# Placing, loading and addressing the expert weights of a mixture of experts in another way

## The chip, the cores and the metric

The kernel runs on one core of one Trainium2 chip. The metric is the device time of one execution in microseconds (us). Engines: PE is TensorE, PEld its weight loads, DVE VectorE, ACT ScalarE, POOL GpSimd, SP SyncE, whose queue issues most transfers.

## The reference, cut to what matters

One layer over 16 meta tokens and 1024 tokens of width 1024: an S5 mixer, an HGRN2 mixer and differential attention side by side, an output projection, and a hierarchical mixture of experts (4 groups of 4 experts, the two best of one group for each token). The change touches only the last:

```python
for e in range(MOE_EXPERTS):                       # 16, of width MOE_FF = 512
    he = jax.nn.silu(t @ w_gate[e]) * (t @ w_up[e])
    y = y + gates[:, e:e + 1] * (he @ w_down[e])   # gates is zero but for two experts of a token
```

All is float32. One expert has 2 MB each of gate, up and down weights.

## The kernel before

**Slots and blocks.** The 2048 pairs of token and chosen expert are sorted by expert into blocks of P = 128 slots, so that a block has one expert and an expert one block or more. The number of blocks depends on the data; the program allows for up to NB, and here 24 run. Functions `..._experts` hold one instruction stream for each engine. `blocks(eng, body)` writes bodies 0 and 1 out, loops over pairs of bodies (j is the pair, par the block in it, b = 2j + par) and writes the last pair out.

**One body.** Body b computes the gate and up products of block b+1 and then the down products of block b. Weights are cut into chunks of 128 rows and 1024 columns: 8 for gate and up (gate and up side by side), 4 for down, so a body has 12 places. float32 products are made of three fp32r products, x_high w_high + x_low w_high + x_high w_low. For each chunk ACT casts the high part (`higher`, L2323), DVE (`lower`, L2375) or POOL (L2220) subtracts it for the low part, and PE (`product`, L2277) does 3 x 2 matmuls of 512 columns. The parts lie in a ring of RING = 4 places; ACT casts a chunk when the chunk four before it has been used (semaphore `chunk_used`). POOL has the last of four chunks (places 3, 7 and 11), DVE the others.

Within a body PE turns the hidden rows (four transposes, L2302), does gate and up, turns the gathered rows of block b+2 (eight transposes, L2257), and does down. ACT then applies SiLU (L2332) and copies the high parts of x (L2328); DVE multiplies gate and up (`hidden`, L2393), takes the low parts of x (L2381) and of the hidden rows (L2442) and scales the outputs of block b-1 (L2401). POOL gathers the rows of block b+2 from DRAM (L2204 and L2207), copies three columns of indices (L2213 to L2215) and adds the outputs of block b-1 into DRAM by a scatter (L2247); DVE's L2401 waits until the scatter before has landed.

**Weights.** There are two places for an expert's weights, `WGU` and `WDN`; an expert that comes new takes the other one. Experts 0 and 1 are loaded ahead. For every block SP reads six table entries: expert, place, whether the expert is new, and three values of `chunk_used` at which the first half of gate and up, the second half and down are free. It then issues five transfers at addresses made of registers, which are skipped where the expert is not new. The other engines that read weights take the places of blocks b and b+1 from a table at the head of each body:

```python
e, q, new, free, free_second, free_down = (sp.value_load(tab[0:1, bass.ds(b, 1)], min_val=0, max_val=hi)
                   for tab, hi in ((eblk, NE - 1), (ebuf, 1), (enew, 1), (efree, 12 * NB), (efree2, 12 * NB), (edown, 12 * NB + 12)))
...
q = buffer_of(eng, b)
return q, (buffer_of(eng, b + 1) if has(par, last, 1) else None)
```

DVE makes the tables in `dve_route` (L2008 to L2041) once the routing is known. The first 8 x 1024 columns of SBUF hold the routing's work and, after the last body, the residual rows.

## Time and profile before

| | us |
|---|---|
| median of 3 runs | 1196.25 |
| the runs | 1192.59 to 1198.74 |
| span of the profiled execution, first to last instruction | 1192.0 |
| experts, body 0 to the end of the last down product | 723.73 to about 1162 |
| PE busy in the span | 1065.8 |
| DVE, ACT, POOL busy | 843.0, 638.6, 487.2 |

The profiled execution is one more execution, of which the trace gives the span and no time of its own; the span is 0.6 us below the fastest run and 4.25 below the median.

How to read the rows: a timeline row has start, time in us, engine, line, operation, output<-input, count; rows of one engine and line that follow closely are merged. In brackets stands the idle time ahead of it and who ended it. A row of windows has start and end, length, then the busy time and instructions of PE, PEld, DVE, ACT and POOL, the granted PE clock as a share of full speed, the mean busy share of the 16 DMA engines and GB/s. A row of a source line has count, then minimum, median and maximum in ns. A row of waits has total us, times, longest.

### The profile page before, as it was taken

To read this page: it belongs to the slowest core of one execution; us is meant where nothing else is said; L and a number is where in the kernel's file an instruction comes from. 1 tells how busy PE (TensorE), PEld (TensorE's weight loads), DVE (VectorE), ACT (ScalarE), POOL (GpSimd) and SP (SyncE) were. 2 spreads that over 40 slices of the span, in tenths; PEclk is the share of its full clock that TensorE was granted. 3 is DMA by queue.
4 is the path that set the end of the run, shared out by engine and by line. 5 is a ranking of instruction groups with operands and counts; after the bars stand their busy time and mean duration, and the time that the engine had idled before them with its cause. 6 is when DMAs were issued, how large, how long until landed. Compare 5 with 4: busy or idle time off the path is not lost. (4 is left out here: it accounts for less than half of the span.)

```text
span 1192.0 us, 22049 instructions
## 1 busy us (share of the span) xinstructions
PE 1065.8 (89%) x7126; PEld 888.2 (75%) x7126; DVE 843.0 (71%) x1234; ACT 638.6 (54%) x1008; POOL 487.2 (41%) x303
## 2 busy tenths in 40 slices
PE   4899998999969989999999648999999999999995
PEld 4898998889968646666667536878777887888873
DVE  5797857563357556555554497888887999899987
ACT  5522111166533456444443326778776887888854
POOL 1121211122000226111111114878775887999960
PEclk9999999999988989999999859999999999999988
DMA  7216434332033820011111774788999878877454
GB/s 266 80 48 73 118 95 127 102 114 71 21 72 80 319 71 1 19 54 53 54 66 59 280 267 159 238 257 305 322 379 371 275 266 286 258 266 229 103 160 161
DMA packets 89495, 194.97 MB, mean 164 GB/s; under 512 B 9265, under 2 KB 32049, under 8 KB 88769
## 3 DMA queue, kind: packets, MB, share of 16 engines
q1 hardware_dynamic: 82800, 169.91, 42.0%
q0 software_dynamic: 6624, 24.12, 8.5%
q8 instruction: 45, 0.74, 0.3%
q14 instruction: 26, 0.20, 0.1%
HBM read 220.60 MB, written 31.51 MB: 211 GB/s over the span
## 5 line engine op out<-in xcount | busy, mean ns | idle before, releaser
L2277 PE MATMUL ps<-split 128*128 128x512 f32 x1728 | 418.1, 398 | 15.8 <-DVE split L2375 8.1
L2277 PEld LDWEIGHTS ps<-split 128*128 128x128 f32 x1728 | 322.4, 190 | 93.3 <-DVE split L2375 12.8
L2323 ACT CAST split<-weights 128x1024 fp32r (+1 forms) x288 | 298.2, 1052 | 101.9 <-PE ps L2277 80.4
L2375 DVE TENSOR_TENSOR split<-weights,split 128x1024 fp32r<-128x1024 f32 x216 | 300.9, 1446 | 46.5 <-ACT split L2323 45.0
L480 PE MATMUL ps<-xsplit,wsplit 128*128 128x384 f32 (+2 forms) x1440 | 239.7, 324 | 4.0 <-POOL wsplit L252 4.0
L2220 POOL TENSOR_TENSOR split<-weights,split 128x1024 fp32r<-128x1024 f32 x72 | 205.0, 2847 | 91.4 <-ACT split L2323 90.4
L480 PEld LDWEIGHTS ps<-xsplit,wsplit 128*128 128x128 f32 x1440 | 226.2, 189 | 5.4 <-POOL wsplit L252 4.6
L252 POOL TENSOR_TENSOR wsplit<-mem,wsplit 128x1024 fp32r<-128x1024 f32 x22 | 57.1, 2597 | 247.7 <-ACT wsplit L335 247.7
L1605 DVE TENSOR_REDUCE sml<-ps 128x1 f32<-128x1040 f32 (+7 forms) x64 | 46.6, 769 | 61.6 <-PE ps L1785 61.6
L1722 ACT COPY mem<-ps 128x512 f32<-128x512 f32 (+3 forms) x48 | 21.4, 481 | 109.3 <-PE ps L1804 71.7
L1548 POOL TENSOR_TENSOR sml<-sml 128x4 f32<-128x4 f32 x8 | 8.1, 1015 | 156.2 <-DVE sml L1626 156.2
L335 ACT CAST wsplit<-mem 128x1024 fp32r<-128x1024 f32 x22 | 23.2, 1053 | 85.1 <-DMA mem<-in_w_in 85.1
L2247 POOL DMA_INDIRECT h_d<-par,sml x22 | 53.0, 2408 | 3.4 <-issue 3.0
L1661 ACT ACTIVATE mem<-ps,sml 128x1040 f32<-128x1040 f32 (+7 forms) x64 | 47.1, 736 | 0.0
L1810 PE MATMUL ps<-mem 128*128 128x128 f32 x288 | 39.3, 282 | 7.1 <-ACT mem L1722 7.1
L2207 POOL DMA_INDIRECT con<-xn_d,sml x24 | 37.7, 1571 | 19.3 <-POOL sml L2204 19.3
L1810 PEld LDWEIGHTS ps<-mem 128*128 128x128 f32 x288 | 34.7, 191 | 12.6 <-ACT mem L1722 12.2
L1785 PE MATMUL ps<-mem 64*128 64x400 f32 (+6 forms) x224 | 42.4, 493 | 0.0
L419 ACT COPY mem<-ps 128x384 f32<-128x384 f32 (+2 forms) x48 | 20.3, 451 | 40.9 <-PE ps L480 34.6
L2328 ACT CAST split<-ps 128x512 fp32r<-128x512 f32 x48 | 25.7, 589 | 17.8 <-PE ps L2257 17.8
L1026 POOL TENSOR_TENSOR sml<-sml 128x16 f32<-128x16 f32 x2 | 7.6, 3800 | 66.6 <-DVE sml L1231 66.6
L2401 DVE TENSOR_SCALAR par<-ps,sml 128x512 f32<-128x512 f32 x44 | 30.9, 744 | 5.1 <-DMA h_d<-par,sml 5.1
(434 smaller groups left out, 1631.1 us busy)
## 6 DMA issues: line engine op xcount, KB each, us to landing
weights<-in_w_down SPq DMA_DIRECT2D x26, 2048.0 KB, 15.9
weights<-in_w_gate SPq DMA_DIRECT2D x50, 1024.0 KB
weights<-in_w_up SPq DMA_DIRECT2D x50, 1024.0 KB
mem<-in_w_in SPq DMA_DIRECT2D x22, 512.0 KB, 4.4
mem<-in_x SPq DMA_DIRECT2D x10, 512.0 KB, 3.5
mem<-in_w_out SPq DMA_DIRECT2D x1, 4096.0 KB, 14.8
h_d<-mem SPq DMA_DIRECT2D x8, 512.0 KB, 2.6
xn_d<-mem SPq DMA_DIRECT2D x8, 512.0 KB, 2.6
```

What stands on the lines that cost most here:

```text
L252: nc.gpsimd.tensor_tensor(WLO[i], RAW[i], WHI[i].bitcast(F32), ALU.subtract).then_inc(wlo_ready, 1)
L480: mm = nc.tensor.matmul(ps[:, n % 6, 0:hi - lo], w[slot_of(h)][:, k % 4, P * m:P * m + P], x[:, k, lo:hi], start=(k == 0 and p_ == 0), sto ...
L1605: nc.vector.tensor_reduce(NMX[:, 2 * (n % 2) + c:2 * (n % 2) + c + 1], logits(c)[:, KEY0:KEY0 + keys_of(n)], AX.X, ALU.max, negate=True).t ...
L1661: f(PR_[n % 2][:, c, 0:nk], logits(c)[:, KEY0:KEY0 + nk], ACT.Exp, bias=NMX[:, o:o + 1], accum_out=SUM[:, o:o + 1]).then_inc(exp_done, 1)
L1785: mm = nc.tensor.matmul(logits(c)[:, s:e], AQ[R, h, P * i:P * i + P], AK[R, h, s - lo:e - lo], start=(e != hi), stop=True, skip_group_chec ...
L1810: nc.tensor.matmul(b[:, 0:P], AT[n % 2][:, k], V[:, 1 + k, vc], start=(k == 0), stop=False)
L2207: pool.indirect_dma_start(XG[:, par], None, xn_d, bass.IndirectOffsetOnAxis(ap=ixc[:, par:par + 1], axis=0)).then_inc(xg_loaded[par], 16)
L2220: nc.gpsimd.tensor_tensor(WL[place % RING], raw(kind, k, q), WH[place % RING].bitcast(F32), ALU.subtract).then_inc(wl_pool, 1)
L2247: pool.indirect_dma_start(h1_d, bass.IndirectOffsetOnAxis(ap=sixc[:, 1 - par:2 - par], axis=0), YE, None, compute_op=ALU.add).then_inc(ye_ ...
L2277: mm = nc.tensor.matmul(ps[:, bank + h, :], x, w[place % RING][:, 512 * h:512 * h + 512], start=(k == 0 and p_ == 0), stop=(k == n - 1 and ...
L2323: nc.scalar.copy(WH[place % RING], raw(kind, k, q)).then_inc(wh_ready, 1)
L2375: nc.vector.tensor_tensor(WL[place % RING], raw(kind, k, q), WH[place % RING].bitcast(F32), ALU.subtract).then_inc(wl_dve, 1)
```

## The change

Gate and up weights get three places, expert e at place e mod 3; the third is the first 8 x 1024 columns of SBUF. Down weights keep two, by parity of e. SP loads every expert's weights in the order of e, at fixed addresses and never skipped: gate and up of e+1, then down of e. It reads one table entry for each expert, the value of `chunk_used` at which half of its gate and up weights have been used in its last block. Every expert gets at least one block.

ACT, DVE and POOL read the place of gate and up from one table (`gtab`, in units of 128 columns) and that of down from another (`dtab`), and ACT the expert (`etab`), since the semaphores of the loads now count experts. DVE and ACT read at the head of a body only where par is 0; the rest is read before place ASK = 6 and place 9, and handed on to the next body in `known`. The first AHEAD = 3 chunks of block 1 are cast and subtracted before the SiLU of block 0.

```diff
 SPLIT = 5 * D + RING * 2 * D
+O_RING = NT * D + 5 * D
+UNIT = 128
+GU_AT = (O_C, O_C + 2 * KD * FF, 0)
...
+        etab, half_free, npair = sml[:, 506:506 + NB].bitcast(I32), sml[:, 398:398 + NE].bitcast(I32), sml[:, 504:505].bitcast(I32)
+        gtab, dtab = sml[:, 570:570 + NB].bitcast(I32), sml[:, 366:366 + NB].bitcast(I32)
         rt_exp, onehot_ready, rank_done, slots_ready, tables_ready, slot_hot_ready, idx_done = (
...
-            link(ts(BLK[:, 0:2], BLK[:, 0:2], 1.0, None, ALU.max))
+            link(ts(BLK, BLK, 1.0, None, ALU.max))
...
-            link(nc.vector.tensor_copy(eblk[:, :], EBF))
-
-            scan = nc.vector.tensor_tensor_scan
-            link(nc.vector.memset(NEW[:, 0:1], 1.0))
-            link(tt(NEW[:, 1:NB], EBF[:, 1:NB], EBF[:, 0:NB - 1], ALU.not_equal))
...
-            link(tt(OLD, OLD, NEW, ALU.subtract))
-            link(scan(BUF, OLD, NEW, 1.0, ALU.mult, ALU.add))
-            link(nc.vector.tensor_copy(ebuf, BUF))
+            link(nc.vector.tensor_copy(etab, EBF))
+            link(tt(ECMP, ECMP, con[:, C_GUB:C_GUB + NE].unsqueeze(1).to_broadcast([P, NB, NE]), ALU.mult))
+            link(red(GUF, ECMP, AX.X, ALU.add))
+            link(ts(GUF, GUF, float(GU_AT[0] // UNIT), None, ALU.add))
+            link(nc.vector.tensor_copy(gtab, GUF))
+            link(ts(PARITY, EBF, 0.5, -0.25, ALU.mult, ALU.add))
...
+            link(nc.vector.tensor_copy(dtab, PARITY))
+            link(tt(PCMP, CB[:, NE - 1:NE].to_broadcast([P, (NB - LEAST) // 2]), con[:, C_IOTAB + LEAST:C_IOTAB + NB:2], ALU.is_gt))
...
+            nc.vector.tensor_copy(half_free, CB).then_inc(tables_ready, 1)
             dve_rows_lower(dve, 0, 0)
-            link(stt(NEW, EBF, 1.5, NEW, ALU.is_gt, ALU.mult))
...
-        WGU = weights[:, 0:4 * KD * FF].rearrange("p (k i n) -> p k i n", i=2, n=FF)
+        WGU = gate_up[:, O_C:].rearrange("p (k i n) -> p k i n", i=2, n=FF)
         WDN = weights[:, 4 * KD * FF:].rearrange("p (k n) -> p k n", n=D)
+        GATE_UP = gate_up[:, :].rearrange("p (a n) -> p a n", n=UNIT)
+        CHUNK = 2 * FF // UNIT
...
-                return WGU[:, bass.ds(q * KD + k, 1)].rearrange("p a i n -> p (a i n)")
+                return GATE_UP[:, bass.ds(q + CHUNK * k, CHUNK)].rearrange("p a n -> p (a n)")
...
+            for half in range(2):
+                sp.sem_inc(w_loads[half], 32)
             sp.wait_ge(xg_loaded[0], 16)
-            sp.dma_start(WDN[:, FF // P:2 * FF // P], a["w_down"][1].rearrange("(k p) n -> p k n", p=P)).then_inc(wdn_loaded, 16)
             sp.wait_ge(first_loaded, 48)
+            sp.sem_inc(wdn_loaded, 16)
+            sp_down(sp, 1)
             sp.wait_ge(tables_ready, 1)
-
-            def body(j, par, first, last):
-                b = 2 * j + par
-                e, q, new, free, free_second, free_down = (sp.value_load(tab[0:1, bass.ds(b, 1)], min_val=0, max_val=hi)
-                                   for tab, hi in ((eblk, NE - 1), (ebuf, 1), (enew, 1), (efree, 12 * NB), (efree2, 12 * NB), (edown, 12 * NB + 12)))
-                for half in range(2):
-                    sp.wait_ge(w_loads[half], 32 * b + 32)
-                    sp.wait_ge(chunk_used, (free, free_second)[half])
-                    for i, w in enumerate(("w_gate", "w_up")):
-                        sp.dma_start(WGU[:, bass.ds(q * KD + 4 * half, 4), i],
-                                     a[w][bass.ds(e, 1), 512 * half:512 * half + 512].rearrange("a (k p) n -> p (a k) n", p=P),
-                                     cond=new).then_inc(w_loads[half], 16)
-                sp.wait_ge(wdn_loaded, 16 * b + 16)
-                sp.wait_ge(chunk_used, free_down)
-                sp.dma_start(WDN[:, bass.ds(q * (FF // P), FF // P)], a["w_down"][bass.ds(e, 1)].rearrange("a (k p) n -> p (a k) n", p=P),
-                             cond=new).then_inc(wdn_loaded, 16)
-
-            return blocks(sp, body)
-
-        def buffer_of(eng, b):
-            return eng.value_load(ebuf[0:1, bass.ds(b, 1)], min_val=0, max_val=1)
-
-        def buffers(eng, b, par, last):
-
-            q = buffer_of(eng, b)
-            return q, (buffer_of(eng, b + 1) if has(par, last, 1) else None)
+            sp.wait_ge(slots_ready, 2)
+            sp_gate_up(sp, 2, None)
+            free = sp_half_free(sp, 0)
+            for e in range(2, NE):
+                if e + 1 < NE:
+                    free_next = sp_half_free(sp, e - 1)
+                    sp_gate_up(sp, e + 1, free)
+                sp_down(sp, e, free)
+                free = free_next
+            pairs = sp.value_load(npair[0:1, 0:1], min_val=0, max_val=(NB - LEAST) // 2) + LEAST // 2
+            return pairs
+
+        def sp_half_free(sp, e):
+
+            return sp.value_load(half_free[0:1, e:e + 1], min_val=12 + gu_used(-1) - KD // 2, max_val=12 * NB)
+
+        def sp_gate_up(sp, e, free):
+
+            for half in range(2):
+                sp.wait_ge(w_loads[half], 32 * e)
+                if free is not None:
+                    if e == 3:
+                        sp.wait_ge(chunk_used, gu_used(0))
+                    sp.wait_ge(chunk_used, free + KD // 2 * half)
+                at = GU_AT[e % 3] + 4 * half * 2 * FF
+                place = gate_up[:, at:at + 4 * 2 * FF].rearrange("p (k i n) -> p k i n", i=2, n=FF)
+                for i, w in enumerate(("w_gate", "w_up")):
+                    sp.dma_start(place[:, :, i], a[w][e, 512 * half:512 * half + 512].rearrange("(k p) n -> p k n", p=P)).then_inc(w_loads[half], 16)
+
+        def sp_down(sp, e, free=None):
+
+            sp.wait_ge(wdn_loaded, 16 * e)
+            if free is not None:
+                sp.wait_ge(chunk_used, free + (down_used(1, False) - gu_used(1) + KD // 2))
+            k = FF // P * (e % 2)
+            sp.dma_start(WDN[:, k:k + FF // P], a["w_down"][e].rearrange("(k p) n -> p k n", p=P)).then_inc(wdn_loaded, 16)
+
+        def expert_of(eng, b):
+            return eng.value_load(etab[0:1, bass.ds(b, 1)], min_val=0, max_val=NE - 1)
+
+        def gate_up_place(eng, b):
+            return eng.value_load(gtab[0:1, bass.ds(b, 1)], min_val=min(GU_AT) // UNIT, max_val=max(GU_AT) // UNIT)
+
+        def down_place(eng, b):
+            return eng.value_load(dtab[0:1, bass.ds(b, 1)], min_val=0, max_val=1)
+
+        ASK = 6
...
-                q, q_next = buffers(pool, b, par, last)
+                q_next = gate_up_place(pool, b + 1) if has(par, last, 1) else None
                 if par and last:
+                    q = down_place(pool, b)
...
+                    if place == KD:
+                        q = down_place(pool, b)
...
+            act.wait_ge(tables_ready, 1)
+            q_first, e_first = gate_up_place(act, 1), expert_of(act, 1)
+            act.wait_ge(w_loads[0], 32 * e_first + 32)
+            act.sem_inc(act_seen, 1)
+            for place in range(AHEAD):
+                higher(0, place, "gu", place, q_first)
             silu(0, 0)
-            act.wait_ge(tables_ready, 1)
             copy_x(1, 1)
 
             def body(j, par, first, last):
                 b = 2 * j + par
-                q, q_next = buffers(act, b, par, last)
+                if par:
+                    e, q_next, e_next, q = known
+                elif first:
+                    q_next, e_next = q_first, e_first
+                else:
+                    q_next, e_next = gate_up_place(act, b + 1), expert_of(act, b + 1)
                 for place, (kind, k) in enumerate(chunks(not has(par, last, 1))):
+                    if first and not par and place < AHEAD:
+                        continue
+                    if place == ASK and has(par, last, 1):
+                        if not par:
+                            e = expert_of(act, b)
+                        q = down_place(act, b)
+                    if place == ASK + 3 and not par:
+                        known[:] = (e_next, None, None, None)
+                        if last:
+                            known[3] = down_place(act, b + 1)
+                        else:
+                            known[1:3] = gate_up_place(act, b + 2), expert_of(act, b + 2)
                     if kind == "gu" and k % 4 == 0:
-                        act.wait_ge(w_loads[k // 4], 32 * b + 96)
+                        act.wait_ge(w_loads[k // 4], 32 * e_next + 32)
                         act.sem_inc(act_seen, 1)
                     if (kind, k) == ("down", 0):
-                        act.wait_ge(wdn_loaded, 16 * b + 32)
+                        act.wait_ge(wdn_loaded, 16 * e + 16)
...
+            q_first = gate_up_place(dve, 1)
+            for place in range(AHEAD):
+                lower(0, place, "gu", place, q_first)
             hidden(0, 0)
             x_lower(1, 1)
             dve_slot_tables(dve, link)
 
             def body(j, par, first, last):
                 b = 2 * j + par
-                q, q_next = buffers(dve, b, par, last)
+                if par:
+                    q_next, q = known
+                else:
+                    q_next = q_first if first else gate_up_place(dve, b + 1)
                 for place, (kind, k) in enumerate(chunks(not has(par, last, 1))):
-                    if place % RING < RING - 1:
+                    if place == ASK and has(par, last, 1):
+                        q = down_place(dve, b)
+                    if place == ASK + 3 and not par:
+                        known[:] = (None, down_place(dve, b + 1)) if last else (gate_up_place(dve, b + 2), None)
+                    if place % RING < RING - 1 and not (first and not par and place < AHEAD):
```

## Rows read from the trace of the kernel before

**Rows 1.** The page, part 1: busy time of TensorE in the span.

```profile
PE 1065.8 (89%) x7126; PEld 888.2 (75%) x7126; DVE 843.0 (71%) x1234; ACT 638.6 (54%) x1008; POOL 487.2 (41%) x303
```

**Rows 2.** Windows, cut where bodies begin, bodies 0 to 21.

```profile
723.73:745.81 22.08, 18.55 (x84) 14.63 (x85) 19.16 (x20) 17.04 (x19) 11.03 (x7) 1.00 0.55 192
745.81:781.91 36.10, 35.99 (x170) 29.30 (x169) 31.70 (x31) 28.52 (x33) 30.92 (x18) 1.00 0.81 272
781.91:801.95 20.04, 18.32 (x85) 14.57 (x84) 16.36 (x16) 14.45 (x17) 13.02 (x10) 1.00 0.70 197
801.95:855.16 53.21, 53.21 (x253) 44.19 (x252) 46.33 (x45) 42.31 (x49) 44.92 (x28) 1.00 0.89 306
855.16:933.90 78.74, 74.33 (x338) 58.00 (x337) 64.06 (x61) 56.18 (x65) 51.88 (x37) 1.00 0.97 340
...
987.50:1008.63 21.13, 18.66 (x86) 14.49 (x85) 19.87 (x17) 14.46 (x17) 14.42 (x10) 1.00 0.96 342
...
sum 409.60, PE 397.36 PEld 321.98 DVE 357.65 ACT 317.73 POOL 325.84; mean PE 49.67 PEld 40.25 DVE 44.71 ACT 39.72 POOL 40.73
```

**Rows 3.** Waits of ScalarE, 704 to 1150 us.

```profile
ACT split L2323 <- DMA weights<-in_w_up: 16.3, 5, 3.8
```

**Rows 4.** Timeline of body 7.

```profile
855.57 0.38 SPq L2185 DMA_DIRECT2D weights<-in_w_down  x1
...
860.52 0.39 SPq L2180 DMA_DIRECT2D weights<-in_w_gate  x1
...
861.16 1.04 ACT L2323 CAST split<-weights 128x1024 fp32r x1 [3.70 <-DMA weights<-in_w_up]
```

**Rows 5.** Source line of SyncE's table reads.

```profile
L2174 SPq TENSOR_LOAD <-sml x144: 261/267/1300, 710.2 to 1101.8; - x144
```

**Rows 6.** Windows: body 8 alone.

```profile
875.07:894.76 19.69, 18.56 (x85) 14.50 (x84) 16.21 (x17) 13.90 (x17) 12.90 (x10) 1.00 1.05 375
```

**Rows 7.** Timeline of ScalarE, end of block 0's gate and up.

```profile
716.77 1.28 ACT L2332 ACT_TABLE_LOAD   x1
721.07 0.60 ACT L2332 ACTIVATE mem<-ps 128x512 f32<-128x512 f32 x1 [3.01 <-PE ps L2277]
...
723.52 1.05 ACT L2323 CAST split<-weights 128x1024 fp32r x1 [0.89 <-issue]
```

**Rows 8.** Timeline of body 0.

```profile
726.32 5.70 DVE L2375 TENSOR_TENSOR split<-weights,split 128x1024 fp32r<-128x1024 f32 x3 [1.44 <-ACT split L2323]
...
727.59 3.04 PE L2277 MATMUL ps<-split 128*128 128x512 f32 x12 [1.73 <-DVE split L2375]
```

**Rows 9.** Source line of VectorE's subtractions.

```profile
L2375 DVE TENSOR_TENSOR split<-weights,split x216: 1208/1218/3432, 685.5 to 1151.9; 128x1024 fp32r<-128x1024 f32 x108
```

**Rows 10.** Timeline of body 14.

```profile
987.02 5.71 DVE L2375 TENSOR_TENSOR split<-weights,split 128x1024 fp32r<-128x1024 f32 x3 [1.35 <-ACT split L2323]
...
989.20 2.44 POOL L2220 TENSOR_TENSOR split<-weights,split 128x1024 fp32r<-128x1024 f32 x1
```

**Rows 11.** Timeline of body 18.

```profile
1061.21 3.50 DVE L2375 TENSOR_TENSOR split<-weights,split 128x1024 fp32r<-128x1024 f32 x3 [1.32 <-ACT split L2323]
...
1063.54 3.44 POOL L2220 TENSOR_TENSOR split<-weights,split 128x1024 fp32r<-128x1024 f32 x1 [0.22 <-ACT split L2323]
```

**Rows 12.** Source line of the other engines' table reads.

```profile
L2191 DVEq FUSED_REGOPS  x69: 65/190/216, 725.2 to 1147.1; - x69
...
L2191 ACTq TENSOR_LOAD <-sml x47: 273/283/1185, 721.9 to 1145.3; - x47
...
L2191 DVEq TENSOR_LOAD <-sml x47: 298/312/1617, 724.6 to 1146.7; - x47
```

**Rows 13.** Timeline of body 3.

```profile
785.96 1.41 DVE L2401 TENSOR_SCALAR par<-ps,sml 128x512 f32<-128x512 f32 x2 [2.03 <-DMA h_d<-par,sml]
```

**Rows 14.** Waits, all engines, 704 to 1140 us.

```profile
PEld ps L2277 <- POOL split L2220: 5.3, 13, 0.6
```

**Rows 15.** Source line of one table operation.

```profile
L2010 DVE TENSOR_SCALAR mem<-mem x1: 181/181/181, 702.6 to 702.6; 128x32 f32<-128x32 f32 x1
```

More of the change, by code:

```diff
@@ L50 @@
 C_TOK, C_DESC4, C_128J, C_SG, C_IOTAB = 896, 912, 928, 936, 937
-C_COS = 976
+C_GUB = 976
+C_COS = 992
 C_SIN = C_COS + L
@@ L90, in constants @@
     c[:, C_IOTAB:C_IOTAB + NB] = np.arange(NB)
+    place = np.array([GU_AT[e % len(GU_AT)] // UNIT for e in range(NE)])
+    c[:, C_GUB:C_GUB + NE - 1] = place[1:] - place[:-1]
     inv = (np.float32(1.0) / (np.float32(10000.0) ** (np.arange(0, 64, 2, dtype=np.float32) / np.float32(64)))).astype(np.float32)
@@ L129, in build @@
             split, weights = split_tensor, weights_tensor
+        with nc.sbuf_tensor("gate_up", [P, O_C + 4 * KD * FF], F32) as gate_up_tensor:
+            gate_up = gate_up_tensor
         with (nc.sbuf_tensor("below_x", [P, O_X], F32), nc.sbuf_tensor("xsplit", [P, 2 * KD * L], F32R) as xsplit_tensor,
@@ L141, in build @@
         MLOE_T = split_at("mix_early_lower", MEM - 512, 512)
+        WHIGH_T, WLOW_T = split_at("weights_higher", O_RING, RING * D), split_at("weights_lower", O_RING + RING * D, RING * D)
         WOL_T = [split_at("wo_lower%d" % k, O_C + 2 * KD * FF + 1024 * k, 1024) for k in range(KD)]
@@ L1878, in build @@
         CB, ECMP, EBF, IXF = take(NE), take(NB, NE), take(NB), take(NB)
-        NEW, OLD, RUN, PRV, BUF, NHALF, NPR = take(NB), take(NB), take(NB), take(NB), take(NB), take(1), take(1)
-        PCMP = take(NB // 2)
+        NPR, PCMP, GUF, PARITY = take(1), take((NB - LEAST) // 2), take(NB), take(NB)
         assert oS <= NT * D
@@ L1886, in build @@
         ixb, ixc = sml[:, 538:538 + NB].bitcast(I32), sml[:, 602:604].bitcast(I32)
-        eblk, ebuf, enew = (sml[:, o:o + NB].bitcast(I32) for o in (506, 570, 398))
-        efree2 = sml[:, 104:104 + NB].bitcast(I32)
-        efree, edown, npair = sml[:, 366:366 + NB].bitcast(I32), sml[:, 334:334 + NB].bitcast(I32), sml[:, 504:505].bitcast(I32)
+        etab, half_free, npair = sml[:, 506:506 + NB].bitcast(I32), sml[:, 398:398 + NE].bitcast(I32), sml[:, 504:505].bitcast(I32)
+        gtab, dtab = sml[:, 570:570 + NB].bitcast(I32), sml[:, 366:366 + NB].bitcast(I32)
         rt_exp, onehot_ready, rank_done, slots_ready, tables_ready, slot_hot_ready, idx_done = (
@@ new lines, in dve_route @@
+            link(ts(GUF, GUF, float(GU_AT[0] // UNIT), None, ALU.add))
+            link(nc.vector.tensor_copy(gtab, GUF))
+            link(ts(PARITY, EBF, 0.5, -0.25, ALU.mult, ALU.add))
+            link(ts(PARITY, PARITY, MAGIC, None, ALU.add))
+            link(ts(PARITY, PARITY, -MAGIC, None, ALU.add))
+            link(nc.vector.scalar_tensor_tensor(PARITY, PARITY, -2.0, EBF, ALU.mult, ALU.add))
+            link(nc.vector.tensor_copy(dtab, PARITY))
+            link(tt(PCMP, CB[:, NE - 1:NE].to_broadcast([P, (NB - LEAST) // 2]), con[:, C_IOTAB + LEAST:C_IOTAB + NB:2], ALU.is_gt))
@@ L2043, in dve_slot_hot @@
+            link(red(NPR, PCMP, AX.X, ALU.add))
+            link(nc.vector.tensor_copy(npair, NPR))
+            link(ts(CB, CB, 12.0, float(gu_used(-1) - KD // 2), ALU.mult, ALU.add))
+            nc.vector.tensor_copy(half_free, CB).then_inc(tables_ready, 1)
+            dve_rows_lower(dve, 0, 0)
         def dve_slot_hot(dve, link):
@@ L2085, in build @@
         HH, HLO = (take_split(FF).rearrange("p (k q) -> p k q", k=FF // P) for _ in range(2))
-        WH, WL = ([take_split(D) for _ in range(RING)] for _ in range(2))
+        WH, WL = ([v[:, r * D:r * D + D] for r in range(RING)] for v in (WHIGH_T, WLOW_T))
+        assert oS == O_RING
+        take_split(2 * RING * D)
         SG, HE = take(FF), take(FF)
@@ L2124, in build @@
         USED0 = 5
+        AHEAD = 3
         def gu_used(b):
@@ L2328, in copy_x @@
                     nc.scalar.copy(XH[:, par, 4 * h:4 * h + 4], ps[:, 6 + h, :].rearrange("p (k q) -> p k q", k=4)).then_inc(xh_ready, 1)
+            known = [None] * 4
             def silu(b, par):
@@ L2422, in tokens_of_slots @@
                                             ALU.is_equal).then_inc(slot_rows_ready, 1)
+            known = [None] * 2
             dve_slot_hot(dve, link)
```

21 lines of the change are left out of this document (removed).

## The prediction

> **What bounds the kernel now.** The page's first part comes first: TensorE is busy for 89% of the span [rows 1]. The change touches only the mixture of experts, so the second view is a table of windows over the first 22 of its 24 bodies (one body per block of 128 slots), cut where the transposes of a body begin [rows 2]. Three bodies in a row took 53.21 us with TensorE busy for all of it: 17.74 us is what a body costs when nothing is late. The 22 bodies from 723.73 to 1133.33 took 409.60 us; 22 x 17.74 = 390.28 would do, and 19.3 us are stalls. They sit in few places: body 0 took 22.08 (4.34 too much), body 3 20.04 (2.30), bodies 7 to 10 78.74 (7.78), body 14 21.13 (3.39). The other fifteen hold the remaining 1.5. That is the most the change can win there, and each piece has a cause of its own.
>
> **Bodies 7 to 10: transfers.** Before its casts ScalarE waited 16.3 us in five pieces for gate and up weights [rows 3]. In body 7 the second half's cast started at 861.16 after 3.70 us of such a wait, and SyncE issued that body's loads, down at 855.57 and the next gate and up at 860.52 [rows 4]. The 5 us between them are register reads, 144 in 24 bodies, six for each [rows 5]. In body 8 the DMA share is full (1.05) at 375 GB/s [rows 6]; 375 GB/s x 19.69 us = 7.4 MB, which is one expert's 6.3 MB with the gathered and scattered rows. Here each expert has one block, so every body needs 7.4 MB, 19.7 us of transfer against 17.74 of work. No order of issue makes that shorter. But the deficit is only 1.95 us a body, 7.8 in four bodies, and the bodies ahead of it have free transfer time (share 0.70 in body 3, 0.89 in bodies 4 to 6 [rows 2]). With a third place, gate and up of expert e+1 wait for expert e-2 and not for e-1: one body, 17.74 us, more lead. 17.74 is more than 7.8, so the whole deficit fits. The static order keeps down(e) behind gate_up(e+1), and down(e) waits for the end of the last body of e-2; it is needed 11.5 us into the first body of e, with singles one body and 11.5 us = 29 us after its release, against 19.7 us for all that is queued with it. I take 0.3 left: minus 7.5 us (bounds 0 and 7.8).
>
> **Body 0: first chunks of block 1 ahead of SiLU.** ScalarE now loads its table at 716.77 while it waits, starts SiLU at 721.07, copies x, and casts the first chunk of the second block at 723.52 after 0.89 us in its sequencer [rows 7]. VectorE's subtractions follow at 726.32, three in 5.70 us, and TensorE stands 1.73 us till 727.59 and again later [rows 8]. After: three casts and three subtractions are done while TensorE still works on block 0, so the 4.34 us go. What is late next is SiLU. A chunk of six matmuls takes (17.74 - 1.0) / 12 = 1.40 us; TensorE's last but one chunk of block 0 ends near 721.0 - 1.4 = 719.6, the third early cast waits for it, starts near 719.9 and ends at 720.95. The table load stands in program order just ahead of SiLU, so its 1.28 us [rows 7] lose their cover: SiLU at 722.25, 1.2 later, and behind it in ScalarE's queue the copies of x, VectorE's lower parts and the transposes. Minus 4.34, plus 1.2: minus 3.1 us (bounds 0, if as much is lost again, and 4.3). The Trainium skill ("ScalarE: Activation LUTs", What ACT_TABLE_LOAD costs) counts a drain of 1.38 us with each load, 2.66 us in all; by it SiLU would come 2.5 late and this part would be worth 1.8. The trace has the load at 1.28 with no such time before it.
>
> **Bodies 3 and 14: two engines in each other's way.** A VectorE subtraction has a median of 1.218 us and a maximum of 3.432 [rows 9]. In body 14 the third one started at 987.02 + 5.71 - 3.43 = 989.30, just after GpSimd's own at 989.20, which took 2.44 [rows 10]: VectorE stood still till GpSimd had finished. In body 18 VectorE's third starts at 1061.21 + 3.50 - 1.22 = 1063.49, GpSimd's at 1063.54 and takes 3.44 [rows 11]; GpSimd is the one that waits and nothing stalls. So every body is a race decided by 0.1 us, and a lost one costs up to 3.4 us; body 0 holds one too (5.70 for three [rows 8]). The Trainium skill ("SBUF — State Buffer", SBUF: two separate sides) says that the first of the two to start keeps a shared port for its whole instruction and the other blocks fully; the trace agrees (3.43 against 1.22 us). Now the reads: ahead of its first subtraction VectorE was idle 1.32 us [rows 11], and its two table reads stand there (a load of 0.31 us and register work of 0.19 each [rows 12]). After the change that place has one read in even bodies and none in odd ones: the race starts 0.5 to 1.1 us earlier, bounded by the third cast, and VectorE wins it. Body 3 was also started by a scatter: VectorE waited 2.03 us for the store of the last rows [rows 13], with the transfers of expert 3 in front of it. Those are issued one body earlier now. I take minus 3.0 for body 14 (bounds 0 and 3.4) and minus 1.8 for body 3 (bounds 0 and 2.3).
>
> **The rest.** GpSimd ended a body's gate and up part too late 13 times, 5.3 us of weight loads waiting in all, most of it overlapped by running matmuls [rows 14]; its column copies are held up by VectorE, which is now earlier. Bodies 1 and 2 keep the 0.6 they lose (36.10 - 35.48, the loop's entry); of the 0.9 us left for bodies 11 to 13 and 15 to 21 I take 0.5. The tables: some 30 small VectorE operations become 18, most at 0.18 us [rows 15]; the path to TensorE's first matmul ends with the x copy, not with them: nothing, either way at most 1 us. SyncE's loads with fixed addresses exist already, at 0.4 us an issue, and nothing waits behind them; conditional ones that were skipped are gone. ScalarE reads more: seven table reads per pair of bodies for four. Each is 0.28 us of load [rows 12], with the register work of VectorE's kind about 0.5; two come between chunks 5 and 6, and the pitch there is 1.40 us with a cast of 1.05 running: they hide under the cast. Zero, bound below.
>
> **Sum.** 7.5 + 3.1 + 3.0 + 1.8 + 0.5 = 15.9 us. The profiled execution spans 1192.0, the three runs lie at 1192.59 to 1198.74 with the median 4.25 above the span; the last instruction to the run's end is not in the trace. 1192.0 - 15.9 = 1176.1 of span, and with the same 4.25 the median is 1180.35, rounded 1180.
>
> **Rivals.**
> The races stay (0.15). New reads sit before chunk 6, where VectorE meets GpSimd's chunk 7; a lost race costs 1.4 to 3.4 us. If bodies 3 and 14 are as before or two others take their place, 4.8 us fewer: 1185. For it: margins under 1 us; against: 0.1 us became more at the place that lost.
> The loads still bind (0.09). If the queue is held by a wait in SyncE's order, such as down(e) in front of gate_up(e+2), the 7.5 us stay: 1188. Against: the lead of 17.74 us over 7.8.
> The opening wins little (0.08): SiLU late by as much as is saved, 3.1 us fewer: 1183.5.
> Slower (0.06): the reads. If ScalarE's two reads, 0.5 us each, are not hidden and shift the cast that GpSimd's slow chunk 7 waits for, that is 1.0 us a body, 22 us: 1180 + 22 = 1202. The point from which it decides is 15.9 / 22 = 0.72 us exposed per body. For it: GpSimd is already the last to finish in 13 bodies; against: four chunks of lead, 4.2 us, in the ring.
> The forecast itself has 0.62.
>
> **Numbers.** Own range of the likeliest case: 1176 to 1185. Below, all 19.3 us gone and a low run: 1174. Above, the race, opening and load rivals: up to 1188, with 2 for the spread of the runs: 1190. 0.5% is 6.0 us, about what can be told from no change: faster means below 1190.3, slower above 1202.2. Faster 0.87, same 0.08, slower 0.05.
>
> **What would show it.** Right: no wait of ScalarE on gate and up weights in bodies 7 to 10, which take 17.7 to 17.9 each; SiLU of block 0 near 722.3, behind its table load, and body 0 at 17.8 to 18.2; at most one subtraction of 3.4 us in places 0 to 2; VectorE's first subtraction under 0.8 us after the x rows. Wrong: transfers at full share in a body over 19 us; idle TensorE after GpSimd's chunk 7 or ScalarE's chunk 6 in every even body.

## The result, and the profile after

The changed kernel takes 1176.1 us (median of 4 runs, 1173.4 to 1178.9) against 1195.4 (median of 4, 1192.6 to 1198.7) in the same session: a ratio of 0.984, 95% interval 0.981 to 0.988. The forecast was 1180, range 1174 to 1190.

Its profiled execution spans 1177.1 us and took 1178.9, the slowest of the four; before's spans 1192.0. The spans differ by 14.9 us, the medians by 19.3. Part of this is the code ahead of the experts, which the diff doesn't touch: the first transposes of gathered rows start at 704.71 in before and at 707.34 in after, and in the profiled executions of the experiments below between 705.7 and 709.9. So I measure **the experts' stretch**, from those transposes to the end of the span. Before it is 1192.0 - 704.71 = 487.3 us, after 1177.1 - 707.34 = 469.8: 17.5 us less.

The windows of the bodies of after, cut as [rows 2] (columns: bounds, length, busy time and instructions of PE, PEld, DVE, ACT and POOL, granted clock, DMA share, GB/s):

```profile
727.35:746.65 19.30, 19.30 (x84) 15.94 (x85) 15.65 (x17) 13.47 (x15) 9.03 (x8) 0.91 0.81 305
746.65:782.06 35.41, 35.41 (x169) 29.48 (x168) 31.26 (x31) 28.91 (x33) 28.36 (x19) 1.00 1.05 388
782.06:799.77 17.71, 17.71 (x85) 14.74 (x84) 14.81 (x16) 14.46 (x17) 12.90 (x10) 1.00 0.82 260
...
852.89:923.75 70.86, 70.86 (x338) 58.99 (x337) 62.24 (x61) 58.09 (x65) 56.85 (x37) 1.00 1.04 382
923.75:1029.96 106.21, 106.21 (x506) 88.40 (x505) 93.36 (x91) 86.80 (x97) 87.70 (x54) 1.00 0.92 315
1029.96:1049.95 19.99, 18.30 (x85) 14.58 (x84) 16.20 (x16) 14.21 (x17) 13.17 (x10) 1.00 0.52 136
1049.95:1120.78 70.83, 70.83 (x338) 58.93 (x337) 63.25 (x61) 57.79 (x65) 59.98 (x35) 1.00 0.44 119
```

Twenty of these 22 bodies take 17.71 us each, without a gap of TensorE. Bodies 7 to 10, in the fifth row, went from 78.74 to 70.86 us while the DMA share is 1.04: the transfers are as dense as before, only earlier. Bodies 3 and 14 are at 17.71 too. Two bodies are left over: body 0 (19.30), where TensorE is busy for all of the time but its clock is 0.91, and body 17 (19.99).

The waits of after, 704 to 1140 us (total, times, longest), beside [rows 3] and [rows 14]:

```profile
DVE par L2449 <- DMA h_d<-par,sml: 9.7, 10, 2.3
...
PEld ps L2301 <- DVE weights_lower L2423: 2.5, 2, 1.9
...
PE ps L2326 <- DVE split L2429: 2.1, 1, 2.1
...
ACT weights_higher L2347 <- DMA gate_up<-in_w_up: 0.2, 1, 0.2
```

ScalarE's 16.3 us of waits for gate and up weights are down to one of 0.2, TensorE's for GpSimd are gone. VectorE's wait for the scatter grew from 5.1 to 9.7 us.

The opening of after: ScalarE's timeline answers to [rows 7].

```profile
719.81 2.20 ACT L2347 CAST weights_higher<-gate_up 128x1024 fp32r x2 [0.61 <-PE ps L2301]
722.31 1.06 ACT L2347 CAST weights_higher<-gate_up 128x1024 fp32r x1 [0.30 <-PE ps L2301]
723.39 1.28 ACT L2358 ACT_TABLE_LOAD   x1
724.68 0.60 ACT L2358 ACTIVATE mem<-ps 128x512 f32<-128x512 f32 x1
```

And the windows of TensorE behind it, same columns as above:

```profile
725.00:727.00 2.00, 0.24 (x5) 0.07 (x2) 1.83 (x4) 2.00 (x4) 0.00 (x0) 1.00 0.68 160
727.00:729.00 2.00, 1.65 (x9) 1.46 (x10) 1.86 (x6) 0.78 (x2) 1.52 (x1) 0.90 0.25 102
729.00:731.00 2.00, 2.00 (x7) 1.54 (x6) 1.75 (x3) 0.91 (x1) 1.27 (x4) 0.50 0.00 0
731.00:733.00 2.00, 2.00 (x8) 1.66 (x7) 1.23 (x1) 0.62 (x2) 0.00 (x0) 0.74 0.61 202
```

The early casts stand ahead of the table load, which now has no cover. TensorE waits 2.1 us for block 1's x rows (0.9 in before), and then runs for about 3 us at half its clock, 1.2 GHz.

Body 17 in the timelines of VectorE and GpSimd:

```profile
1033.99 1.41 DVE L2449 TENSOR_SCALAR par<-ps,sml 128x512 f32<-128x512 f32 x2 [2.28 <-DMA h_d<-par,sml]
1035.32 0.68 DVE L2501 TENSOR_TENSOR split<-ps,split 128x512 fp32r<-128x512 f32 x1
1035.91 5.69 DVE L2423 TENSOR_TENSOR weights_lower<-gate_up,weights_higher 128x1024 fp32r<-128x1024 f32 x3
...
1037.57 2.95 POOL L2241 TENSOR_TENSOR weights_lower<-gate_up,weights_higher 128x1024 fp32r<-128x1024 f32 x1 [2.92 <-ACT weights_higher L2347]
```

VectorE waits 2.28 us for the scatter of the block before, comes to its three subtractions late, and the third starts while GpSimd's is running: 5.69 us for three, as in [rows 10], here at places 4 to 6. Before's body 3 lost its race at place 6 too, behind the same kind of wait [rows 13]: that race was not gone, it had moved to another body.

### The profile page after: what moved, and what is told of

The parts are those of the page before. It is cut to its first block and busy times, and to the rows that moved or that the text cites. A ratio compares the mean times of both kernels' runs of the same rounds, so it can differ in the third digit from the quotient of the medians.

```text
span 1177.1 us, 21252 instructions
## 1 busy us (share of the span) xinstructions
PE 1062.5 (90%) x7126; PEld 895.1 (76%) x7126; DVE 833.9 (71%) x1221; ACT 643.1 (55%) x1008; POOL 473.1 (40%) x303
## 3 DMA queue, kind: packets, MB, share of 16 engines
q1 hardware_dynamic: 82800, 169.92, 41.4%
HBM read 157.69 MB, written 31.51 MB: 161 GB/s over the span
## 5 line engine op out<-in xcount | busy, mean ns | idle before, releaser
L2301 PE MATMUL ps<-weights_higher,split 128*128 128x512 f32 x1152 | 317.0, 397 | 3.0 <-DVE split L2501 2.3
L2301 PEld LDWEIGHTS ps<-weights_higher,split 128*128 128x128 f32 x1152 | 215.5, 190 | 46.7 <-issue 2.6
L2347 ACT CAST weights_higher<-gate_up 128x1024 fp32r (+1 forms) x192 | 200.6, 1056 | 53.9 <-PE ps L2301 48.8
L2423 DVE TENSOR_TENSOR weights_lower<-gate_up,weights_higher 128x1024 fp32r<-128x1024 f32 x144 | 178.8, 1288 | 15.6 <-ACT weights_higher L2347 14.3
L2301 PE MATMUL ps<-weights_lower,split 128*128 128x512 f32 x576 | 180.0, 394 | 1.7 <-DVE weights_lower L2423 1.7
L2241 POOL TENSOR_TENSOR weights_lower<-gate_up,weights_higher 128x1024 fp32r<-128x1024 f32 x48 | 119.1, 2482 | 76.8 <-ACT weights_higher L2347 75.5
L2301 PEld LDWEIGHTS ps<-weights_lower,split 128*128 128x128 f32 x576 | 109.4, 190 | 26.0 <-DVE weights_lower L2423 2.5
L2423 DVE TENSOR_TENSOR weights_lower<-weights,weights_higher 128x1024 fp32r<-128x1024 f32 x72 | 109.5, 1572 | 26.7 <-ACT weights_higher L2347 26.7
L2347 ACT CAST weights_higher<-weights 128x1024 fp32r x96 | 101.3, 1055 | 31.2 <-PE ps L2301 30.1
L2241 POOL TENSOR_TENSOR weights_lower<-weights,weights_higher 128x1024 fp32r<-128x1024 f32 x24 | 64.1, 2670 | 13.9 <-ACT weights_higher L2347 13.4
L1819 PE MATMUL ps<-mem 128*128 128x128 f32 x288 | 39.3, 282 | 7.1 <-ACT mem L1731 7.1
```

The source lines that it names most:

```text
L1819: nc.tensor.matmul(b[:, 0:P], AT[n % 2][:, k], V[:, 1 + k, vc], start=(k == 0), stop=False)
L2241: nc.gpsimd.tensor_tensor(WL[place % RING], raw(kind, k, q), WH[place % RING].bitcast(F32), ALU.subtract).then_inc(wl_pool, 1)
L2301: mm = nc.tensor.matmul(ps[:, bank + h, :], x, w[place % RING][:, 512 * h:512 * h + 512], start=(k == 0 and p_ == 0), stop=(k == n - 1 and ...
L2347: nc.scalar.copy(WH[place % RING], raw(kind, k, q)).then_inc(wh_ready, 1)
L2423: nc.vector.tensor_tensor(WL[place % RING], raw(kind, k, q), WH[place % RING].bitcast(F32), ALU.subtract).then_inc(wl_dve, 1)
```

## Experiments

Each row: median, ratio to before with its interval, experts' stretch of the profiled execution, and the bodies that took over 18.3 us. The runs behind one median spread over 2 to 13 us. The stretch leaves out the code ahead of the experts, but it comes from one execution of each kernel, and how far it varies between executions is not shown. Body 5 shows that it can: it takes 19.46 us in e8 and 17.7 in after, e2 and e3, though e8 differs from these in the opening alone.

| kernel | us | ratio | stretch | long bodies |
|---|---|---|---|---|
| before | 1195.4 | | 487.3 | 0, 2, 3, 7 to 10, 14 |
| after | 1176.1 | 0.981 to 0.988 | 469.8 | 0, 17 |
| e1 two places | 1181.0 | 0.982 to 0.992 | 474.1 | 0, 7, 9, 10 |
| e2 nothing ahead | 1178.3 | 0.982 to 0.990 | 469.7 | 0, 17 |
| e3 table early | 1176.7 | 0.977 to 0.988 | 469.4 | 17 |
| e4 reads at head | 1188.0 | 0.992 to 0.997 | 480.5 | 0, 4, 5, 13, 16, 17, 19 to 21 |
| e5 before, GpSimd waits | 1218.1 | 1.011 to 1.022 | 510.7 | 18 of 22 |
| e6 after, GpSimd waits | 1184.3 | 0.988 to 0.996 | 477.4 | 3, 5, 7, 17 |
| e7 both of e3, e6 | 1184.1 | 0.989 to 0.994 | 476.8 | 3, 5, 17 |
| e8 table early, nothing ahead | 1177.9 | 0.980 to 0.990 | 470.3 | 0, 5, 17 |
| e9 scatter first | 1174.1 | 0.977 to 0.987 | 467.3 | 0 |
| e10 scatter and table | 1170.1 | 0.975 to 0.983 | 464.4 | none |
| e11 VectorE's reads at head | 1178.2 | 0.981 to 0.991 | 475.2 | 0, 5, 17, 20 |
| e12 ScalarE's reads at head | 1190.1 | 0.993 to 0.999 | 483.1 | 0, 4, 5, 13, 16, 17, 19 to 21 |

**Is it the third place, or the static issue?**

```diff
-GU_AT = (O_C, O_C + 2 * KD * FF, 0)
+GU_AT = (O_C, O_C + 2 * KD * FF)
...
+                sp_down(sp, e, free)
                 if e + 1 < NE:
                     free_next = sp_half_free(sp, e - 1)
-                    sp_gate_up(sp, e + 1, free)
-                sp_down(sp, e, free)
+                    sp_gate_up(sp, e + 1, free_next)
...
-                at = GU_AT[e % 3] + 4 * half * 2 * FF
+                at = GU_AT[e % 2] + 4 * half * 2 * FF
```

> The kernel after, with its gate and up weights back in two places (block e in place e mod 2, loads still static and in the order down(e), then gate and up (e+1), each behind the product that frees its place). If the third place is what removed the stalls of bodies 7 to 10, those four bodies and body 3 go back from 17.7 us to 19 to 20 us each, ScalarE or GpSimd or VectorE wait for their transfers again, and the kernel is 6 to 9 us slower than after. If the gain came from the static issue without register reads on SyncE, the bodies stay at 17.7 us and the time is within 1 us of after.

4.9 us slower than after in the medians. ScalarE's waits in it, 704 to 1140 us:

```profile
ACT weights_higher L2347 <- DMA gate_up<-in_w_up: 11.8, 7, 5.0
```

Bodies 7, 9 and 10 take 21.60, 19.48 and 18.74 us, 6.7 more than in after; body 3 stays at 17.71. e1 still issues its loads at fixed addresses and without the reads, so what makes bodies 7 to 10 short is the third place with the order of transfers that goes with it, not the static issue. For bodies 3 and 8 (17.71 too) the expectation failed.

**What did casting ahead bring?** e2 sets AHEAD = 0. e3 loads the table early, e8 does both:

```diff
             copy_x(0, 0)
+            nc.scalar.activation(SG[:, 0:1], con[:, C_ONES:C_ONES + 1], ACT.Silu)
```

> The kernel after, with no chunks of the second block cast ahead of SiLU. If casting ahead is what shortened body 0, that body goes back from 19.3 us to about 22 us, the table load and SiLU come about 2 us earlier, and the total is 1.5 to 3 us longer than after. If casting ahead paid little, because TensorE's wait for SiLU and the lower granted clock behind it (0.91 over body 0) took back what it gave, the total is within 1 us of after.

> The kernel after, with a SiLU of one column, of constants, put on ScalarE behind its first x copy, so that the table is loaded while TensorE still has products of block 0 to do. If TensorE's 2.1 us of idle before the first hidden transposes is what lets its clock fall, the 1.28 us of table load leave that wait, it is 0.8 to 1.0 us, the granted clock of body 0 is 1.00 and the body takes 17.8 us instead of 19.3: 2.5 to 3 us less in all. If the clock falls for another reason, body 0 stays at 19.3 us and only up to 1.2 us are won.

> The kernel after, with the table loaded early and no chunks cast ahead. If casting ahead pays 2 us once the granted clock holds, the stretch from the first x transposes to the end of body 0 takes 39 us here, against 37.3 us with both, 39.3 us in after and 39.2 us with neither. If the early table alone made the gain and the casts ahead pay nothing, it takes 37 to 38 us.

From the first transposes to the end of body 0: before 41.1 us, after 39.3, e2 39.2, e8 39.2, e3 37.3. Body 0 of e3, and of e2:

```profile
729.47:747.17 17.70, 17.70 (x85) 14.76 (x85) 14.73 (x17) 13.47 (x15) 8.22 (x8) 1.00 0.85 321
```

```profile
726.90:747.43 20.53, 18.32 (x84) 14.61 (x85) 19.43 (x20) 16.04 (x18) 10.55 (x7) 1.00 0.94 348
```

Without casts ahead VectorE's race of [rows 8] is back (5.70 us for three subtractions) and body 0 takes 20.53; with them it is 19.3, but the late SiLU and the clock take it all back. With the table loaded early both are avoided and the casts ahead are worth 1.9 us. The early table alone (e8 against e2) brings nothing. e3 failed in one point: TensorE's wait fell only from 2.10 to 1.85 us, not to 0.9, since VectorE's three subtractions ahead (ending at 727.5) now hold its own multiplication back. In the stretch e3 is only 0.4 us shorter than after, because its body 17 took 21.58 us and not 19.99; the medians don't tell the two apart.

Why body 0 of e2 is 1.5 us shorter than that of before, I did not test.

**Whose reads matter?** e4 puts all table reads of ScalarE and VectorE back at the head of each body, e11 VectorE's alone, e12 ScalarE's alone. For ScalarE:

```diff
-                if par:
-                    e, q_next, e_next, q = known
-                elif first:
+                q, e = down_place(act, b), expert_of(act, b)
+                if first and not par:
                     q_next, e_next = q_first, e_first
-                else:
+                elif has(par, last, 1):
                     q_next, e_next = gate_up_place(act, b + 1), expert_of(act, b + 1)
...
```

> The kernel after, with all table reads of ScalarE and of VectorE back at the head of each body (GpSimd's stay where they are). If spreading them is what lets VectorE start its subtraction ahead of GpSimd's, VectorE's first subtraction of a body begins about 1.3 us later, some bodies show its 3.4 us form in places 0 to 2 and take 19 to 21 us, and the total is 1 to 7 us longer. If the place of the reads doesn't matter, all bodies stay at 17.7 us and the time is within 0.5 us of after.

> The kernel after, with the table reads of VectorE alone back at the head of its bodies. With both engines' reads there it was 12 us slower than after. If VectorE's late first subtraction, coming under GpSimd's, is the cost, most of it stands here: 8 to 12 us slower than after, with bodies of 18 to 20 us. If ScalarE's late first cast is the cost, this kernel is within 2 us of after.

> The kernel after, with the table reads of ScalarE alone back at the head of its bodies. If VectorE's late first subtraction is the cost of the kernel with both, this one is within 2 us of after; if ScalarE's late first cast is, which makes VectorE and GpSimd late together, it is 8 to 12 us slower.

e4 is 12 us slower than after, more than expected. e12 alone is 14 us slower (stretch 13.3 more), e11 2 us (stretch 5.4 more, by body 20 at 21.05 above all). So most of the cost of e4 comes by ScalarE's reads and not, as I had expected, by VectorE's. But e12 is no return to before: it has four reads of ScalarE at the head, where before had two. e11 does take VectorE back to before's two reads, and its body 20 is before's body 14 over again:

```profile
1084.67 2.01 ACT L2347 CAST weights_higher<-gate_up 128x1024 fp32r x2 [0.18 <-issue]
...
1087.36 5.77 DVE L2423 TENSOR_TENSOR weights_lower<-gate_up,weights_higher 128x1024 fp32r<-128x1024 f32 x3 [1.38 <-ACT weights_higher L2347]
...
1089.63 2.42 POOL L2241 TENSOR_TENSOR weights_lower<-gate_up,weights_higher 128x1024 fp32r<-128x1024 f32 x1 [1.23 <-ACT weights_higher L2347]
```

Body 14 of before, ScalarE's casts and VectorE's table reads (both ahead of its subtraction at 987.02 [rows 10]):

```profile
984.22 2.01 ACT L2323 CAST split<-weights 128x1024 fp32r x2 [0.19 <-issue]
```

```profile
L2191 DVEq TENSOR_LOAD <-sml x2: 309/792/1274, 984.5 to 986.2; - x2
```

The brackets name ScalarE's cast as what ended VectorE's wait, 1.35 and 1.38 us. But a cast takes 1.05 us: the first one had ended at 985.27 in before and at 1085.72 in e11, and VectorE began 1.75 and 1.64 us after that. In before its second read started at 986.2 and took 0.31 us, with register work of 0.19 behind it. VectorE was late by its own reads in both. Over bodies 1 to 21 its first subtraction starts this long after the end of ScalarE's first cast: before 0.2 to 2.0 us (median 0.8), e11 0.25 to 1.6 (0.8), after 0.15 to 0.6 (0.15), e12 0.15 to 0.16. In e12 it is the cast that VectorE waits for. Body 4 of e12, in the timelines of the three engines:

```profile
801.43 3.90 ACT L2347 CAST weights_higher<-gate_up 128x1024 fp32r x4 [2.61 <-PE ps L2301]
...
802.64 3.50 DVE L2412 TENSOR_TENSOR weights_lower<-gate_up,weights_higher 128x1024 fp32r<-128x1024 f32 x3 [2.17 <-ACT weights_higher L2347]
...
805.60 2.80 POOL L2241 TENSOR_TENSOR weights_lower<-gate_up,weights_higher 128x1024 fp32r<-128x1024 f32 x1 [2.71 <-ACT weights_higher L2347]
...
808.36 1.17 POOL L2234 COPY sml<-sml 128x1 int32 x1
...
811.76 2.41 POOL L2241 TENSOR_TENSOR weights_lower<-gate_up,weights_higher 128x1024 fp32r<-128x1024 f32 x1
...
814.34 2.39 POOL L2271 DMA_INDIRECT h_d<-par,sml  x1 [0.17 <-issue]
```

And body 4 of after, then its body 5, which has no reads at its head:

```profile
796.82 3.02 ACT L2347 CAST weights_higher<-gate_up 128x1024 fp32r x3 [0.50 <-issue]
...
798.49 3.50 DVE L2423 TENSOR_TENSOR weights_lower<-gate_up,weights_higher 128x1024 fp32r<-128x1024 f32 x3 [0.82 <-ACT weights_higher L2347]
...
813.90 2.28 ACT L2347 CAST weights_higher<-gate_up 128x1024 fp32r x2
815.13 3.87 DVE L2423 TENSOR_TENSOR weights_lower<-gate_up,weights_higher 128x1024 fp32r<-128x1024 f32 x3
```

ScalarE stands 2.61 us between its x copies and its first cast in e12 (the last of its four reads end just before that cast; the name PE is only the last semaphore). In after it is 0.50 us in body 4 and nothing in body 5. The delay reaches GpSimd's subtraction at place 3, then everything behind it in GpSimd's queue: three column copies, the subtraction at place 7, the scatter. The scatter lands later, and VectorE waits for it in the body after.

**Would VectorE ahead of GpSimd be enough?** e5 adds a wait to before, e6 to after, e7 to e3.

```diff
+                if b is not None and place in (RING - 1, 2 * RING - 1) and kind == "gu":
+                    pool.wait_ge(wl_dve, counts(b, place - 1)[1] + 1)
```

> The kernel before, with one wait more on GpSimd: its subtraction at places 3 and 7 also waits until VectorE has done the one of the place ahead, so that VectorE never comes second. If the 3.4 us form of VectorE's subtraction, started under GpSimd's, is what made bodies 0, 3 and 14 long, they lose 2 to 3 us each and the kernel is 5 to 8 us faster than before, with bodies 7 to 10 unchanged at 19.5 to 19.9 us. If VectorE's late start itself is the cost, the bodies stay as they are or GpSimd becomes the one that PE waits for, and the time is within 1 us of before or longer.

> The kernel after, with the same wait on GpSimd. If body 17 is long because VectorE, held 2.3 us by the scatter, starts its subtraction under GpSimd's, body 17 goes from 20.0 us to under 18.5 us, no VectorE subtraction of one chunk takes 3.4 us, and the kernel is 1.5 to 2.5 us faster than after. If holding GpSimd back costs as much in other bodies, they go above 17.71 us and the total is within 0.5 us of after or longer.

> The kernel after, with the table loaded early (as in the kernel that has that alone) and GpSimd's wait for VectorE. Both losses that are left in the expert stage should be gone: body 0 at 17.7 us, body 17 under 18.5 us, 4 us less than after in all, so about 1172 us. If body 17 stays long whatever GpSimd does, or the granted clock falls all the same, 1174 to 1177 us.

The rivals won: e5 is 22 us slower than before, e6 and e7 are 8 us slower than after. Waits of e6, 735 to 1120 us:

```profile
POOL weights_lower L2243 <- DVE weights_lower L2425: 43.4, 41, 4.3
...
PEld ps L2303 <- POOL weights_lower L2243: 12.1, 19, 1.7
```

VectorE's subtractions of gate and up chunks take at most 2.03 us in it, and yet the bodies get longer: TensorE's weight loads wait 12.1 us for GpSimd. GpSimd has no slack for a wait. So the lost race is where an engine's lateness shows; making the other one late as well does not cure it.

**What makes body 17 long?** e9 issues the scatter at place 3 and copies the columns at place 7; e10 has the early table too.

```diff
-                    if place == RING - 1 and not (par and last):
-                        if not first:
-                            pool.wait_ge(ye_stored, 16 * b - 16)
-                        columns(b, par, False)
-                    if place == 2 * RING - 1 and (par or not first):
+                    if place == RING - 1 and (par or not first) and not (par and last):
                         pool.wait_ge(ye_copied, 2 * b)
...
+                    if place == 2 * RING - 1 and not (par and last):
+                        if not first:
+                            pool.wait_ge(ye_stored, 16 * b - 16)
+                        columns(b, par, False)
```

> The kernel after, with GpSimd's scatter of the last block's outputs put behind its subtraction at place 3 instead of behind the one at place 7, and the three small column copies at place 7 in its stead. In after, VectorE waits 2.3 us in body 17 for the scatter of the block before. If that wait is what makes its subtraction come second and the body long, VectorE's waits for the scatter are gone, body 17 takes under 18 us and the kernel is 2 to 2.5 us faster than after. If the two engines get in each other's way there for another reason, or the scatter's 2.4 us of GpSimd ahead of place 7 make that subtraction late, the body stays at 20 us or others lengthen, and the time is within 0.5 us of after or longer.

> The kernel after, with the early scatter and the table loaded early. If both losses that are left go, body 0 takes 17.7 us and body 17 under 18 us: 4 us less than after, about 1172 us. If only the early table works, about 1174 us.

In e9 VectorE has no wait for the scatter left and body 17 takes 17.71 us. The copies moved with the scatter, so e9 shows what the two moves do together. The windows of e10, body 0 and bodies 1 to 21:

```profile
729.62:747.35 17.73, 17.73 (x85) 14.77 (x86) 14.74 (x17) 13.53 (x15) 10.89 (x8) 1.00 0.85 324
747.35:1119.20 371.85, 371.85 (x1766) 309.40 (x1765) 334.87 (x316) 303.23 (x337) 315.26 (x188) 1.00 0.82 281
```

TensorE is busy without a gap: 389.6 us for 22 bodies, the ideal that the prediction set at 390.3. e10 takes 1170.1 us (median of 6), ratio 0.979 to before, and beats both kernels in the stretch (464.4 against 469.8). Against after alone the medians differ by 6.0 us with intervals that overlap (0.975 to 0.983, and 0.981 to 0.988).

## Why the prediction was right, and where it was not

**Bodies 7 to 10 (-7.5).** Measured -7.88 (78.74 to 70.86). Undoing the place gave back 6.7 in these bodies. Right in cause and size.

**Opening (-3.1 = -4.34 + 1.2).** Measured -1.8. The stretch up to body 0 went from 19.02 to 20.01 us, +1.0 for the 1.2 of the uncovered table load: right. Body 0 went from 22.08 to 19.30, -2.8 and not -4.34. The stalls are gone as the step said; the 1.6 us left are TensorE at half clock behind its 2.1 us of idle, which the step did not count: it took the late SiLU as 1.2 us of delay and nothing else. The Trainium skill's 2.66 us for a table load ("ScalarE: Activation LUTs", What ACT_TABLE_LOAD costs) does not show: the load of 1.28 us starts 0.02 after the cast before it, SiLU 0.01 after it. That the part came out at 1.8, as it would by those 2.66 us, is chance: SiLU is 1.0 late and not 2.5, and the rest is the clock.

**Bodies 14 and 3 (-3.0, -1.8).** Measured -3.4 and -2.3. For body 14 the step was right in size and in cause. "Ahead of its first subtraction VectorE was idle 1.32 us, and its two table reads stand there": ScalarE's first cast had been done for 1.75 us when VectorE began in body 14 of before, and in after VectorE begins 0.15 us behind it. The time from VectorE's x rows to its subtraction fell by 0.87 us there, from 1.35 to 0.48, within the 0.5 to 1.1 of the step. Putting VectorE's two reads back (e11) brought the collision back, at 21.05 us for 21.13, though in body 20 and in one execution. What the step did not have is ScalarE: four reads ahead of its first cast cost 14 us (e12), more than all that VectorE's do, and they make VectorE and GpSimd late together. For body 3 the size was right and the cause is open. Its race was lost at place 6, behind the wait for the scatter [rows 13], and in after VectorE still waits there, but for 1.34 us and not 2.03:

```profile
784.85 1.41 DVE L2449 TENSOR_SCALAR par<-ps,sml 128x512 f32<-128x512 f32 x2 [1.34 <-DMA h_d<-par,sml]
```

The step put this down to transfers that the third place lets be issued a body earlier. e1 has no third place, waits 1.50 us there and has body 3 at 17.71, so that was not needed; no run had the scatter alone late.

**The rest (-0.5).** Bodies 1 and 2, which were to keep their 0.6, lost 0.7; the other bodies lost their small excess, 1.3 in all; body 17 took 2.24 back. Together bodies 1 to 21 went from 387.5 to 374.1 us, -13.4, where 7.5 + 4.8 + 0.5 = 12.8 was forecast. The rival "the races stay" came true in that one body. The rival named new reads ahead of chunk 6 as the starter; what is seen is the late scatter, and ahead of that a late ScalarE: in body 16 its first cast came after 1.21 us of idle, for 0.50 in body 4, and one table read at the head of that body took 1.33 us, for a median of 0.285 (the row is that body's alone):

```profile
L2209 ACTq TENSOR_LOAD <-sml x1: 1327/1327/1327, 1008.0 to 1008.0; - x1
```

In e9, where that gap is 0.16 us, body 17 is short, but e9 moves the scatter too. Body 20 of after has the same slow read and nothing follows. So the read as the starter of body 17 is not shown.

**The signs named.** SiLU at 724.68 is 722.05 on before's clock (the experts began 2.63 later), for 722.3. No subtraction in places 0 to 2 takes 3.4 us. VectorE's first subtraction comes within 0.15 us of the x rows in the odd bodies, but after more than the 0.8 named in bodies 2, 4, 6, 16, 18, 20 and 22 (0.82 to 1.46). Body 0 at 17.8 to 18.2 did not come.

**Not foreseen.** From body 22 to the end: 58.67 to 56.32, -2.35 us. The down products of block 23 ran at half clock for less time: granted clock 0.57 in their first 7 us in before, 0.76 in after, whose window is

```profile
1140.50:1147.50 7.00, 6.97 (x24) 5.57 (x24) 5.45 (x8) 0.49 (x2) 1.54 (x1) 0.76 1.00 373
```

An estimate from these rows: 7 x (0.76 - 0.57) = 1.3 us of the 2.35 are the clock, 0.5 the shorter wait ahead of them (2.86 to 2.35), 0.3 body 22. Why the clock fell for less time is not known (below). Sum: -1.8 - 13.4 - 2.35 = -17.5, against 15.9. That the sum came so near is in part luck: the opening missed by 1.3 and this part was not in the forecast.

**From span to median.** The 4.25 us between before's span and its median were carried over as if they belonged to the kernel. In every run whose span is on record, of after and of all the others, the time is 1.7 to 1.9 us above the span. So some 2.4 of the 4.25 only say that before's profiled execution was quicker than its median run (an estimate: 1192.0 + 1.8 = 1193.8, where the median was 1196.25). After's took 1178.9, 2.8 above its median, so that there the median lies 1.0 below the span. From 1180.35 to 1176.1 it is -1.6 for the larger sum, +2.6 for the later start of the experts in that execution, and -5.25 for the offset (from +4.25 to -1.0): -4.25. This offset was the term of the sum that was furthest off, and the later start hid half of it. The two profiled spans differ by 14.9 us; the other 4.4 of the 19.3 between the medians come from which executions were profiled.

## What to carry to other kernels

When an engine has an idle gap, the profile names the last semaphore that it waited for. Look at when that work had ended: here the named cast had been done for 1.75 us in before, and the engine's own table reads filled the gap; in body 4 of e12 it had been done for 0.16 us, and the engine had indeed waited for it. Putting back one engine's reads at a time tells the two apart. Where two engines block each other, ask which of them is late and why: making one wait for the other cost 8 to 22 us here, moving the late scatter ahead removed the collision. Work moved into a gap can uncover what was hidden there, here a table load of 1.28 us; move that too.

## What the runs showed of the hardware

- TensorE's clock fell to half in body 0 of after and of every other kernel there with a 2.1 us wait before it but one (e1, e4, e9, e11 and e12 too; not e6, window clock 1.00), and in none with 1.9 us or less (e2, e3, e7, e8, e10). Before block 23's down products it fell after 2.34 us in e3, 2.46 in e9 and 2.86 in before, and did not after 2.46 in e10 or 2.87 in e4. The length of the idle time alone does not decide it. A fall cost 1.6 us in body 0, and 1.1 us ahead of block 23's down products (from body 22 to the end, 56.25 us in e9 with it and 55.16 in e10 without).
- Small copies share in the blocking: GpSimd's 128x1 copies take 0.18 us, and 1.17 to 1.20 while VectorE subtracts. Three of them made 3.5 us of GpSimd's time in a body. The Trainium skill ("SBUF — State Buffer", SBUF: two separate sides) has a port that the two share and that one of them holds for its whole instruction; these copies agree with it.
- The page of the profile counts skipped transfers as reads of memory. Before's reads are 220.60 MB and after's 157.69, while the queue moved 169.9 MB in 82800 packets in both. The difference, 62.9 MB, is ten times an expert's 6.29 MB, and ten experts' loads were skipped in before (26 issues of down weights there, 16 in after). After's row:

```profile
HBM read 157.69 MB, written 31.51 MB: 161 GB/s over the span
```

- A table read into a register takes 0.28 us on ScalarE and 0.31 on VectorE in the median, but single ones took over 1 us (1.27 on VectorE in body 14 of before, 1.33 on ScalarE in body 16 of after).
- A DMA share of 1.05 with 388 GB/s in bodies 1 and 2 of after costs TensorE nothing: it has no gap there.
